# Norm sums of squares as one 512-column product per chunk with 32 columns of ones, the root taken in row form, and five of eight sums moved into the last slab

## The reference

```python
def rmsnorm(x, g):
    xf = x.astype(jnp.float32)
    y = xf * lax.rsqrt(jnp.mean(xf * xf, axis=-1, keepdims=True) + EPS)
    return (y * g.astype(jnp.float32)).astype(x.dtype)

def swiglu(h, w_in, w_out):
    gate, up = jnp.split(h @ w_in, 2, axis=-1)
    return (jax.nn.silu(gate) * up) @ w_out
```

## Time and profile before

| | us |
|---|---|
| median of 3 runs (lowest to highest) | 2110.55 (2108.54 to 2113.11) |
| the profiled execution's own time | 2112.95 |
| its span | 2111.0 |
| PE busy | 1997.0 (95%) |
| PEld busy | 1598.9 (76%) |
| DVE busy | 941.1 (45%) |
| ACT busy | 737.9 (35%) |
| POOL busy | 705.5 (33%) |

### The profile page before, as it was taken

The page is one execution under the profiler, slowest core; times in us unless marked ns, Lnnn a source line. Parts: engine busy times, 40 slices in busy tenths (PEclk is TensorE's granted clock), DMA queues, the critical chain, the costliest instruction groups (busy, mean ns, idle before and its releaser), DMA issues.

```text
span 2111.0 us, 25872 instructions
## 1 busy us (share of the span) xinstructions
PE 1997.0 (95%) x10132; PEld 1598.9 (76%) x10136; DVE 941.1 (45%) x1361; ACT 737.9 (35%) x1203; POOL 705.5 (33%) x296
## 2 busy tenths in 40 slices
PE   6999988888999999999999999888999989999998
PEld 3788756777888888788888877755876778888886
DVE  2551577754444430434443334666776532222102
ACT  3423355433222221422222134536256433222212
POOL 1322100323444444334444433310421334444442
PEclk8999998879999999999999999999999999999999
DMA  8661110002344452334445522200211222322321
GB/s 328 216 251 50 41 60 1 21 31 100 133 146 149 157 182 90 111 120 139 146 156 182 189 66 90 70 30 21 90 57 35 80 81 80 100 94 94 100 89 60
DMA packets 60126, 223.61 MB, mean 106 GB/s; under 512 B 6800, under 2 KB 7056, under 8 KB 58256
## 3 DMA queue, kind: packets, MB, share of 16 engines
q1 hardware_dynamic: 59472, 220.13, 30.4%
q10 hardware_dynamic: 576, 2.43, 0.3%
HBM read 220.43 MB, written 2.10 MB: 105 GB/s over the span
## 4 chain that ended last, share of the span: by engine, by line
PE 84%; DVE 9%; ACT 3%; issue 2%; DMA 1%; SPq 0%; DVEq 0%; ACTq 0%
PE ps L425 72%; PE ps L564 2%; DVE hl L630 2%; DVE t L638 1%; DMA raw<-stream 1%; PE ps L979 1%; DVE neg_max L1124 1%; PE ps L2299 1%; PE ps L2128 1%; PE ps L2290 0%; PE ps L2320 0%; PE ps L998 0%; PE ps L2150 0%; PE ps L901 0%; PE ps L2308 0%
## 5 line engine op out<-in xcount | busy, mean ns | idle before, releaser
L1745 POOL TENSOR_TENSOR w_lo<-raw,w_hi 128x1024 fp32r<-128x1024 f32 x276 | 666.2, 2414 | 1322.8 <-ACT w_hi L438 719.2
L425 PE MATMUL ps<-hh,w_hi 128*128 128x512 f32 (+1 forms) x1512 | 604.1, 400 | 29.3 <-DVE hl L630 20.3
L425 PE MATMUL ps<-hh,w_lo 128*128 128x512 f32 (+1 forms) x1512 | 594.2, 393 | 0.0
L425 PE MATMUL ps<-hl,w_hi 128*128 128x512 f32 (+1 forms) x1512 | 594.2, 393 | 0.0
L425 PEld LDWEIGHTS ps<-hh,w_hi 128*128 128x128 f32 (+1 forms) x1512 | 286.8, 190 | 103.6 <-issue 32.0
L425 PEld LDWEIGHTS ps<-hh,w_lo 128*128 128x128 f32 (+1 forms) x1512 | 286.5, 189 | 62.1
L425 PEld LDWEIGHTS ps<-hl,w_hi 128*128 128x128 f32 (+1 forms) x1512 | 287.0, 190 | 57.5
L1718 ACT ACTIVATE w_hi<-raw 128x1024 fp32r<-128x1024 f32 x126 | 133.7, 1061 | 472.1 <-PE ps L425 472.1
L491 DVE SCALAR_TENSOR_TENSOR mod_raw<-mod_raw,cond_ada 128x1024 f32<-128x1024 f32 x72 | 116.6, 1621 | 249.3 <-DMA mod_raw<-late 249.3
L425 PE MATMUL ps<-act_hi,w_hi 128*128 (+1 forms) x528 | 209.3, 396 | 0.0
L425 PE MATMUL ps<-act_lo,w_hi 128*128 (+1 forms) x528 | 209.3, 396 | 0.0
(11 more groups left out here) (417 smaller groups left out, 2352.6 us busy)
## 6 DMA issues: line engine op xcount, KB each, us to landing
raw<-stream SPq DMA_DIRECT2D x284, 512.0 KB, 3.4
mod_raw<-late SPq DMA_DIRECT2D x72, 512.0 KB, 4.5
early_raw<-early SPq DMA_DIRECT2D x32, 512.0 KB, 5.7
mod_w<-mod_w SPq DMA_DIRECT2D x8, 1024.0 KB, 14.7
xT<-xT SPq DMA_DIRECT2D x2, 1024.0 KB, 14.7
xT<-xT ACTq DMA_DIRECT2D x2, 1024.0 KB, 6.0
out<-fin SPq DMA_DIRECT2D x8, 256.0 KB, 2.2
csta<-csta SPq DMA_DIRECT2D x1, 1344.0 KB, 20.8
```

What stands on the lines that cost most here:

```text
L425: mm = pe.matmul(out, w, r, start=first and i == 0, stop=last and i == 2)
L1745: pool.tensor_tensor(lo[:, :], raw[n % RING][:, :], hi[:, :].bitcast(F32), ALU.subtract)\
```

## The change

`norm_sum` becomes, for every norm but `nc` (`BY_TILE`), one fp32 matmul per chunk: 32 columns of ones are the weights and the 512 squares of the chunk the moving side, into partitions 0 to 31 of the bank. The sums now stand as rows. ACT takes the root of 32x512 values into `sq[0]` (`std_row`), PE turns four 32x128 pieces into 128x32 with transposes into the same bank (new key `_std`, freed by `rs`), and DVE takes the reciprocal from that bank instead of from `std`. The broadcast transposes of `rs` behind that are as before. `ffn_tensor` gets the name of the norm behind it and, in its last slab, puts the sum of chunk m-3 behind the three matmuls of output chunk m (`SLAB_LAG`), so five sums lie in the last slab; three stay behind. These sums use bank 0, which DVE's first residual addition frees.

```diff
+    ROW = 32
+    BY_TILE = ("nc",)
+    std_row = sq[0]
     def norm_sum(pe, key, k, chunks, tokens, ba):
         if k == 0:
             norm_starts(key, chunks)
             claim(pe, ba, key + "_ss")
         pe.wait_ge(*norm(key, "sq", k + 1))
+        if key not in BY_TILE:
+            mm = pe.matmul(ps[0:ROW, ba, 0:tokens], c("one").broadcast_to([P, ROW]), sq[k % 2][:, 0:tokens], start=(k == 0),
+                           stop=(k == chunks - 1))
+            mm.then_inc(S("norm_sq_used") if k < chunks - 1 else bank_full(ba), 1)
+            return
...
         for k in range(first, chunks):
             norm_sum(pe, key, k, chunks, tokens, ba)
+        if key not in BY_TILE:
+            claim(pe, ba, key + "_std", norm(key, "rs", 1))
+            for t in range(tiles):
+                mm = pe.transpose(ps[:, ba, t * ROW:(t + 1) * ROW], std_row[0:ROW, t * P:(t + 1) * P], c("ident")[0:ROW, 0:ROW])
+            mm.then_inc(bank_full(ba), 1)
         claim(pe, bb, key + "_rs", norm(key, "t1", chunks))
...
     def norm_root(act, key, tokens, width):
         b = full(act, key + "_ss")
-        act.activation(std[key][:, :], ps[:, b, 0:tokens:P], ACT.Sqrt, bias=c("eps"), scale=1.0 / width).then_inc(bank_empty(b), 1)
+        if key in BY_TILE:
+            act.activation(std[key][:, :], ps[:, b, 0:tokens:P], ACT.Sqrt, ...)
+        else:
+            act.activation(std_row[0:ROW, 0:tokens], ps[0:ROW, b, 0:tokens], ACT.Sqrt, bias=c("eps")[0:ROW, :], scale=1.0 / width)\
+               .then_inc(bank_empty(b), 1)
...
     def norm_vector(dve, key, src, chunks, tokens, gains, hi, lo, shift, out=None):
-        read(dve, key + "_ss")
-        dve.reciprocal(rs[key][:, :], std[key][:, :]).then_inc(S("norm_rs"), 1)
+        if key in BY_TILE:
+            ...
+        else:
+            b = full(dve, key + "_std")
+            dve.reciprocal(rs[key][:, :], ps[:, b, 0:ROW * (tokens // P):ROW]).then_inc(S("norm_rs"), 1)
...
+    SLAB_LAG = 3
-    def ffn_tensor(pe, key, key_norm, name_in, name_out):
+    def ffn_tensor(pe, key, key_norm, name_in, name_out, sums_of):
...
                 if last:
                     mm.then_inc(bank_full(m), 1)
+                    if m >= SLAB_LAG:
+                        norm_sum(pe, sums_of, m - SLAB_LAG, KD, N, 0)
...
-        norm_tensor(pe, "nf1", KD, N, 4, 5)
+        norm_tensor(pe, "nf1", KD, N, 0, 5, KD - SLAB_LAG)
```

More of the change, by code:

```diff
@@ L591, in norm_root @@
         b = full(act, key + "_ss")
-        act.activation(std[key][:, :], ps[:, b, 0:tokens:P], ACT.Sqrt, bias=c("eps"), scale=1.0 / width).then_inc(bank_empty(b), 1)
+        if key in BY_TILE:
+            act.activation(std[key][:, :], ps[:, b, 0:tokens:P], ACT.Sqrt, bias=c("eps"), scale=1.0 / width).then_inc(bank_empty(b), 1)
+        else:
+            act.activation(std_row[0:ROW, 0:tokens], ps[0:ROW, b, 0:tokens], ACT.Sqrt, bias=c("eps")[0:ROW, :], scale=1.0 / width)\
+               .then_inc(bank_empty(b), 1)
     def norm_high(act, key, k, tokens, hi, shift):
@@ L603, in norm_scalar @@
                 norm_square(act, key, src, k, tokens, ready)
-        b = full(act, key + "_ss")
-        act.activation(std[key][:, :], ps[:, b, 0:tokens:P], ACT.Sqrt, bias=c("eps"), scale=1.0 / width).then_inc(bank_empty(b), 1)
+        norm_root(act, key, tokens, width)
         if hi is None:
@@ L619, in norm_vector @@
     def norm_vector(dve, key, src, chunks, tokens, gains, hi, lo, shift, out=None):
-        read(dve, key + "_ss")
-        dve.reciprocal(rs[key][:, :], std[key][:, :]).then_inc(S("norm_rs"), 1)
+        if key in BY_TILE:
+            read(dve, key + "_ss")
+            dve.reciprocal(rs[key][:, :], std[key][:, :]).then_inc(S("norm_rs"), 1)
+        else:
+            b = full(dve, key + "_std")
+            dve.reciprocal(rs[key][:, :], ps[:, b, 0:ROW * (tokens // P):ROW]).then_inc(S("norm_rs"), 1)
         b = full(dve, key + "_rs")
@@ L2639, in _ @@
         norm_tensor(pe, "n2", KD, N, 4, 5, KD - SUM_LAG)
-        ffn_tensor(pe, "ffn1", "n2", "w_ffn_in", "w_ffn_out")
-        norm_tensor(pe, "nf1", KD, N, 4, 5)
-        ffn_tensor(pe, "ffn2", "nf1", "w_ffn1_in_2", "w_ffn1_down_2")
-        norm_tensor(pe, "nm", KD, N, 4, 5)
+        ffn_tensor(pe, "ffn1", "n2", "w_ffn_in", "w_ffn_out", "nf1")
+        norm_tensor(pe, "nf1", KD, N, 0, 5, KD - SLAB_LAG)
+        ffn_tensor(pe, "ffn2", "nf1", "w_ffn1_in_2", "w_ffn1_down_2", "nm")
+        norm_tensor(pe, "nm", KD, N, 0, 5, KD - SLAB_LAG)
         proj2_tensor(pe)
@@ L2652, in _ @@
         norm_tensor(pe, "nf2", KD, N, 4, 5, KD - SUM_LAG)
-        ffn_tensor(pe, "ffn3", "nf2", "w_ffn2_in_2", "w_ffn2_down_2")
-        norm_tensor(pe, "nfin", KD, N, 4, 5)
+        ffn_tensor(pe, "ffn3", "nf2", "w_ffn2_in_2", "w_ffn2_down_2", "nfin")
+        norm_tensor(pe, "nfin", KD, N, 0, 5, KD - SLAB_LAG)
     @block.scalar
```

## The result

The changed kernel takes 2117.96 us (median of 15 runs, 2115.62 to 2124.79) against 2112.99 of the kernel before, measured beside it (median of 15, 2108.54 to 2114.78). The ratio is 1.0031, 95% interval 1.0022 to 1.0039, so 4.6 to 8.2 us slower. Forecast was slower, by 10.5 us, 2121.0. The direction was right, the size about 4 us too large.

A forecast was written before the change was run, and what follows sets the result against it. PE, busy 95% of the span, was taken to bound the kernel, plus the last sum's latency path; 6.2 + 2.6 - 0.3 + 2.0 + 0 = +10.5 us on 2110.55 gave 2121.0 us, range 2113 to 2128.

The forecast's parts named there:

- Price of a new sum between products: Each 32-column sum between PE's products costs 1.16 us (0.86 to 1.25), 0.26 more than the old sum.
- n2 and nf2: Stages before these norms: ten sums between products at 0.26 more, +2.6 us; the last two sums shorter, -0.3 us.
- The slab: Last slab before nf1, nm, nfin: from 8.03 to 8.70 us, +0.67 each, +2.0 us; moving sums removes no PE work.
- The root path: Root's start to first broadcast transpose, seven norms: 0.62 to 1.51 us, +0.89 each, +6.2 us (+5.0 to +8.3).
- nx: Norm at the start: its part costs nothing, since the chain stands on a weight transfer until 33.6 us.
- ncq and nckv, sums: Sums of these two norms, on a slow clock: zero change, between -0.5 and +0.5 us together.
- Nothing covers it: Added root latency, +0.89 us per norm, counts in full because PE's, DVE's and ACT's next instructions wait for it.
- Rival 1: Within the noise: switches cost nothing extra, each sum 0.86, only the root path's low end remains; about 2113.5 us; chance 0.14.
- Rival 2: Faster: a single 32-column product in the five large norms costs, say, 0.43 us; about 2100 us; chance 0.05.
- Rival 3: Clock falls already within the final chain of sums: 14 us more, about 2135, or 2128 if midway; chance 0.11.

The follow-up runs named there:

- wide: The changed kernel with 128 instead of 32 columns of ones in the row sums; ratio 1.0010 against the kernel before, 2.1 us slower.
- whole_third: The changed kernel, unedited, run a third time; ratio 1.0048 against the kernel before, 10.1 us slower.
- nx_rows: The kernel before with row sums and turned root for nx alone; ratio 1.0001 against the kernel before.
- recip_rows: As wide, but ACT roots all 128x512, DVE inverts in place and PE turns nothing; ratio 1.0119 against the kernel before, 25 us slower.
- second and third sample: The changed kernel, unedited, timed again twice beside the kernel before; ratios 1.0033 and 1.0048.
- slab_alone: The kernel before with only the move of five sums into the last slab, sums and roots by tiles; ratio 0.9989, 0.4 to 4.0 us faster.

## Why the prediction was right, and where it was not

- **Price of a new sum between products**: predicted 1.16, measured 1.16 to 1.17; additions before n2 at 3.92, before nf2 at 6.78 us instead of 6.52. Its parts hold too: without the switch of tile shape (`wide`) it is 0.86. The prediction's rows 7 show no weight load; that the narrow weights come late is seen at 480.21.
- **n2 and nf2**: predicted 2.6 - 0.3 = +2.3; measured +1.15 from the first addition to n2's root, and nf2's stage adds the same 0.26 per step.
- **The slab**: predicted +0.67 a layer. Measured n2 to nf1 +1.61, less 0.91 for n2's root path: +0.70. The end of the last products to the root took 4.1, as predicted. That the move removes no PE work was right for row sums; for tile sums it saved 0.3.
- **The root path**: predicted 1.51 us and +0.89, measured 1.53 and +0.91. The time of the path held to 0.02, partly by luck: the ACT root took 0.68, 0.08 more than the nearest row gave, and the hand-over to PE 0.05 instead of 0.10; the turn took 0.43. In one profile (whole_third) nckv's path ran at a clock of 0.50 and took 1.73.
- **nx**: predicted free; `nx_rows` shows it free within 2 us.
- **ncq and nckv, sums**: predicted 0 (-0.5 to +0.5 together); the chain of waits of the first pair of profiles shows 4.56 to 4.39 and 3.77 to 3.23, so -0.7. Most of the second difference is the clock, granted at 0.59 over nckv's row sums in that profile and at 0.51 in the kernel before. In the third profile of the changed kernel it was 0.50, and nckv's sums took 3.63 from start to root against 3.79; ncq's took 4.41 against 4.58 at 0.63 in both kernels. At equal clock the gain is about 0.3 together.
- **The term that was mis-sized** is the root path of nf1 and nm, "Nothing covers it": +0.89 each predicted, +0.41 measured from the root to the first product (4.34 to 4.75). ACT splits the next weights behind the root, POOL follows, and in both kernels POOL's pass is still running when DVE starts the first `hl`. Timeline of the kernel before:
```profile
869.79 1.05 ACT L438 ACTIVATE w_hi<-raw 128x1024 fp32r<-128x1024 f32 x1
...
870.92 2.36 POOL L1745 TENSOR_TENSOR w_lo<-raw,w_hi 128x1024 fp32r<-128x1024 f32 x1 [10.89 <-ACT w_hi L438]
...
872.45 1.38 DVE L630 SCALAR_TENSOR_TENSOR hl<-t,ada,hh 128x512 fp32r<-128x512 f32 x1
```
and of the changed kernel:
```profile
868.35 1.04 ACT L438 ACTIVATE w_hi<-raw 128x1024 fp32r<-128x1024 f32 x1
...
869.47 2.35 POOL L1770 TENSOR_TENSOR w_lo<-raw,w_hi 128x1024 fp32r<-128x1024 f32 x1 [12.05 <-ACT w_hi L438]
...
871.50 0.87 DVE L651 SCALAR_TENSOR_TENSOR hl<-t,ada,hh 128x512 fp32r<-128x512 f32 x1
```
`hl` takes 0.75 alone. Here it takes 1.38 and 0.87, and in both it ends 0.55 us behind POOL's pass: 873.83 behind 873.28, 872.37 behind 871.82. So what sets the first product is POOL's end, and that moved only by what ACT's longer root moved the split (0.16 behind the root before, 0.58 after: 0.42). The turn and the second hand-over are hidden behind POOL. Two comparisons bear this out. In n2 and nf2 no POOL pass lies there, `hl` takes 0.75 in both kernels, and the first product comes 0.91 and 0.90 later. In `recip_rows` the chain is so late that POOL has ended before `hl` begins, and `hl` takes 0.75 in nf1:
```profile
877.70 2.34 POOL L1768 TENSOR_TENSOR w_lo<-raw,w_hi 128x1024 fp32r<-128x1024 f32 x1 [10.77 <-ACT w_hi L438]
...
881.64 0.75 DVE L649 SCALAR_TENSOR_TENSOR hl<-t,ada,hh 128x512 fp32r<-128x512 f32 x1
```
It also fits nf1 to nm: 0.91 + 0.70 - 0.51 = 1.10, measured 1.06 to 1.15.
- **The sum again**, with measured prices: 7 x 0.91 + 1.15 + 1.2 + 3 x 0.70 - 1.0, less 0.3 to 0.7 for ncq's and nckv's sums, is 9.1 to 9.5 us, against 10.5 predicted and 7.4 (6.5, 7.0, 10.1) timed. That the size came out below the forecast is thus explained for 1 to 1.4 us. The other 2 or so stay open. The intervals of the second and third sample reach up to 9.7 and 13.3, that of the first only to 8.2. The stretches with many short PE pieces, whose length depends on PE's clock, differ by over 4 us within one kernel and could hold them, but nothing shows that they do: the stretch to the first addition has a mean of 464.2 in the four profiles with the old root in n2 and the norms behind it (both of the kernel before, `nx_rows`, `slab_alone`) and of 464.4 in the seven with row roots and fp32 sums.
- **Rival 1** lost its mechanism: a narrow product between wide ones does cost 0.30 more, as `wide` shows. **Rival 2** (cheap narrow products) is refuted by 0.97 for each. **Rival 3** (the clock falls within the final chain) did not occur: four sums took 3.67 us in every profile of the whole change, at 0.90 a step. Its other half, that a slow stretch behind a gap is nearly free, holds, though rows 9 show one execution only. Windows of the first two us of products behind n2, in the kernel before and in its second profile:
```profile
495.16:497.16 2.00, 2.00 (x9) 1.57 (x10) 1.97 (x3) 0.72 (x1) 0.00 (x0) 1.00 0.00 0
```
```profile
490.59:492.59 2.00, 2.00 (x5) 1.61 (x6) 1.97 (x3) 0.72 (x1) 0.00 (x0) 0.50 0.00 0
```
The clock is 1.00 in one and 0.50 in the other, and n2's root to nf1's takes 378.25 and 378.29.

## What to carry to other kernels

Price a product by what it streams and by what stands around it: 32 columns instead of 128 saved nothing on TensorE here, and the excursion to the narrow shape between dense products, late weight load included, cost 0.30 us each time. Moving work to another place in the list of the engine that bounds the kernel gains only what that engine was waiting. A reduction that ends in a serial chain over engines pays each added hop in full, unless a pass of another engine ends later: then only what moves that pass counts. What a sum streams (0.86 us in fp32, 0.23 in fp32r) was worth more here than any order of the same work.

## What the runs showed of the hardware that was not expected

- DVE's reciprocal takes 3.36 us for 128x512 fp32, 6.5 ns a column, while a multiply of the same shape takes 0.75.
- DVE's `hl` (0.75 us alone) ends 0.55 us behind a POOL pass of 128x1024 that is running when it starts: it takes 1.38 with 0.83 of POOL left, 0.87 with 0.32 left.
- A 128-column fp32 product placed between 128x128 products costs its stream alone, 0.86 us for 512 columns; with 32 columns it costs 1.16.
- A PE stretch of seven score records took 2.91 or 1.54 us in two executions of one program, with the granted clock at 0.64 and then 0.50 in the first and 1.00 in the second. Two profiles of a kernel with many short PE stretches can differ by 4 to 5 us in one stretch while its dense stretches agree to 0.05.
